# Between two sublayers of a decoder trunk: squares summed on four column groups of TensorE and folded, and the second half's root laid among the first half's features

## The reference, cut to what matters

```python
def rmsnorm(x, g):
    y = x * lax.rsqrt(jnp.mean(x * x, axis=-1, keepdims=True) + NORM_EPS)
    return y * g

x = x + 0.5 * rmsnorm(swiglu(rmsnorm(x, gains[0]), ...), gains[1])
x = x + rmsnorm(mixer(rmsnorm(x, gains[2])), gains[3])
x = x + 0.5 * rmsnorm(swiglu(rmsnorm(x, gains[4]), ...), gains[5])
```

## Time and profile before

| | us |
|---|---|
| median of 3 runs (2783.35 to 2790.81) | 2788.54 |
| the profiled execution | 2786.83 |
| its span | 2785.2 |
| PE busy in it | 2673.0 (96%) |
| DVE busy | 1274.3 (46%) |
| ACT busy | 855.1 (31%) |
| POOL busy | 427.5 (15%) |

### The profile page before, as it was taken

The page is one execution under the profiler, slowest core; times in us unless marked ns, Lnnn a source line. Parts: engine busy times, 40 slices in busy tenths (PEclk is TensorE's granted clock), DMA queues, the critical chain, the costliest instruction groups (busy, mean ns, idle before and its releaser), DMA issues.

```text
span 2785.2 us, 52286 instructions
## 1 busy us (share of the span) xinstructions
PE 2673.0 (96%) x20733; PEld 2511.4 (90%) x20733; DVE 1274.3 (46%) x2112; ACT 855.1 (31%) x1415; POOL 427.5 (15%) x616
## 2 busy tenths in 40 slices
PE   7999999999888999999999999999999889999998
PEld 6999998977444999999899999899999878999998
DVE  5444226554544444432444442468435555544423
ACT  2222223233432332222332232334333233322221
POOL 3000003011443100000100000255144442000001
PEclk9999999999999999999999999999989999999999
DMA  4233322222997222332123333133110114233321
GB/s 116 83 90 88 102 75 69 77 68 72 332 339 264 61 83 84 90 103 84 56 85 89 89 97 94 44 84 83 46 36 1 31 47 129 77 89 90 103 84 43
DMA packets 397671, 263.03 MB, mean 94 GB/s; under 512 B 10954, under 2 KB 370583, under 8 KB 397497
## 3 DMA queue, kind: packets, MB, share of 16 engines
q1 hardware_dynamic: 386012, 223.03, 27.4%
q0 software_dynamic: 11536, 38.28, 4.1%
HBM read 251.71 MB, written 9.56 MB: 94 GB/s over the span
## 4 chain that ended last, share of the span: by engine, by line
PE 90%; DVE 5%; issue 1%; ACT 1%; DMA 1%; POOL 1%; SPq 0%; DVEq 0%; POOLq 0%; ACTq 0%
PE ps L486 67%; PE ps L472 5%; PE ps L2247 2%; PE ps L2268 1%; PE ps L1369 1%; PE ps L2265 1%; PE ps L1381 1%; PE ps L1421 1%; PE ps L500 1%; PE ps L1312 1%; PE ps L1330 1%; PE ps L527 1%; PE ps L1313 1%; PE ps L2231 1%; PE ps L2489 1%
## 5 line engine op out<-in xcount | busy, mean ns | idle before, releaser
L464 DVE TENSOR_TENSOR w_lo<-w_raw,w_hi 128x1024 fp32r<-128x1024 f32 (+1 forms) x314 | 419.8, 1337 | 957.9 <-ACT w_hi L457 956.6
L486 PE MATMUL ps<-hd_hi,w_hi 128*128 128x272 f32 x3712 | 774.7, 290 | 6.0 <-DVE w_lo L464 6.0
L486 PE MATMUL ps<-hd_lo,w_hi 128*128 128x272 f32 x3712 | 767.9, 288 | 0.0
L486 PE MATMUL ps<-hd_hi,w_lo 128*128 128x272 f32 x3712 | 764.1, 287 | 0.0
L457 ACT CAST w_hi<-w_raw 128x1024 fp32r<-128x1024 f32 (+1 forms) x314 | 351.1, 1118 | 1088.6 <-PE ps L486 1023.0
L486 PEld LDWEIGHTS ps<-hd_hi,w_hi 128*128 128x128 f32 x3712 | 581.4, 189 | 14.7 <-issue 14.3
L486 PEld LDWEIGHTS ps<-hd_lo,w_hi 128*128 128x128 f32 x3712 | 584.7, 189 | 0.0
L486 PEld LDWEIGHTS ps<-hd_hi,w_lo 128*128 128x128 f32 x3712 | 582.3, 189 | 0.0
L967 POOL TENSOR_TENSOR xT<-xT,rstd_rows 128x272 f32<-128x272 f32 x96 | 81.0, 871 | 1709.4 <-DVE rstd_rows L992 1709.4
L486 PE MATMUL ps<-h_hi,w_hi 128*128 128x272 f32 x1232 | 255.3, 289 | 0.0
L486 PE MATMUL ps<-h_lo,w_hi 128*128 128x272 f32 x1232 | 254.7, 288 | 0.0
(11 more groups left out here) (500 smaller groups left out, 3175.6 us busy)
## 6 DMA issues: line engine op xcount, KB each, us to landing
w_raw<-in_ffn_w_gate_dram SPq DMA_DIRECT2D x88, 512.0 KB, 3.8
w_raw<-in_ffn_w_up_dram SPq DMA_DIRECT2D x88, 512.0 KB, 3.8
w_raw<-in_ffn_w_down_dram SPq DMA_DIRECT2D x64, 704.0 KB, 4.5
k_pages<-in_cache_a_k_dram SPq DMA_DIRECT2D x128, 256.0 KB, 4.6
v_pages<-in_cache_a_v_dram POOLq DMA_DIRECT2D x128, 256.0 KB, 4.5
w_raw<-in_c_w_in_dram SPq DMA_DIRECT2D x33, 512.0 KB, 4.1
w_raw<-in_ab_w_in_dram SPq DMA_DIRECT2D x25, 512.0 KB, 3.9
w_raw<-in_ab_w_out_dram SPq DMA_DIRECT2D x8, 512.0 KB, 3.7
```

The costliest lines, as they stand in the source:

```text
L464: e.tensor_tensor(w_lo[:, n % 2, 0:nk * P], raw[:, n % RAW, 0:nk * P], w_hi[:, n % 2, 0:nk * P].bitcast(F32), ALU.subtract).then_inc(sem(" ...
L486: mm = e.matmul(ps[:, bank + h, 0:TH], w, x[:, k0 + k, half(h)], start=first and k == 0 and w is wh and x is x_hi, stop=last and k == nk - ...
```

## The change

1. The squares of the new `x` are no longer summed feature by feature by a 128-column product. After features 3 and 7 of a half, four products with 32 columns of ones each go to the four column groups of PE (`ps[j * 32:(j + 1) * 32]`), one for each feature. The four groups' partial sums are copied to scratch by DVE (`dve_sums_out`) and added by one full product (`folded`), after feature 4 of half 1 for half 0, and inside the second unit of half 1 for half 1. The mean divides by 32 times more, since each row of a group is there 32 times.
2. ACT writes squares into six strips instead of two, and waits on PE only at squares 6, 10 and 14 of the 16, and at square 2 for `y_summed` (the strips hold y's squares until then).
3. The last sums of y (`pe_last_sums`) stand in `pe_head`, behind the three passes of feature 0, except after the sixth sublayer.
4. The 12 operations of the second half's root are laid among `scaled` and `x_low` of features 2 to 4 (`dve_rstd_step`), four for each, and wait for each other one by one. Its diagonal stands after `x_low` in feature 5, `pe_rows(1)` after feature 5 instead of 4. This holds for the last turn too.
5. The second unit's `w_hi` stands after feature 4 on ACT and its `w_lo` after feature 6 on DVE.

On DVE, at the first place between sublayers, before: from the `scaled` of feature 4 on (`rstd_rows<-y_ffn` is `scaled`, `hd_lo` is `x_low`, `w_lo` the split of the weights, `small` the root).

```diff
@@ -354,6 +354,10 @@
     return scr[:, x // 2, half(x % 2)]
+def square_strip(h, k):
+    return strip((0, 2, 1, 3, 4, 5)[(h * KD + k) % 6])
@@ -495,10 +499,17 @@
     base = 2 * KD * s
-    def squares(h, k):
-        e.wait_ge(sem("x_squared"), base - 2 * KD + h * KD + k + 1)
-        e.matmul(ps[:, 4 + h, 0:TH], ones[:, :], strip(2 * (k % 2)), start=k == 0, stop=k == KD - 1,
-                 skip_group_check=True).then_inc(sem("squares_summed"), 1)
+    def squares(h, g):
+        e.wait_ge(sem("x_squared"), base - 2 * KD + h * KD + 4 * g + 4)
+        for j in range(4):
+            mm = e.matmul(ps[j * 32:(j + 1) * 32, 4 + h, 0:TH], ones[:, 0:32], square_strip(h, 4 * g + j), start=g == 0,
+                          stop=g == 1, skip_group_check=True)
+        mm.then_inc(sem("squares_summed"), 1)
+    def folded(h):
+        e.wait_ge(sem("sums_copied"), 2 * s - 1 + h)
+        e.matmul(ps[:, 4 + h, 0:TH], ones[:, :], strip(6 + h), start=True, stop=True,
+                 skip_group_check=True).then_inc(sem("squares_folded"), 1)
...
                 if at == 0:
                     e.wait_ge(sem("hd_lo_ready"), base + h * KD + k + 1)
                 mm = pe_passes(e, n, k, hd_hi, hd_lo, k, bank, h, k == 0, k == KD - 1)
-                if at == 0 and s:
-                    squares(h, k)
-                if at == 0 and h == 0 and k == 4 and s:
+                if at == 0 and h == 0 and k == 0 and s:
+                    pe_last_sums(e, s - 1)
+                if at == 0 and k in (3, 7) and s:
+                    squares(h, k // 4)
+                if at == 0 and h == 0 and k == 5 and s:
                     pe_rows(e, s - 1, 1)
+                if h == 1 and at == 0 and k == 4 and s:
+                    folded(0)
+                if h == 1 and at == 1 and k == 3 and s:
+                    folded(1)
             if h == 1:
                 mm.then_inc(sem("unit_done"), 1)
             if h == 1 and at == 0 and between:
@@ -529,6 +546,12 @@
                           skip_group_check=True)
     if last:
         mm.then_inc(sem("y_summed"), 1)
+def pe_last_sums(e, s):
+    g = out_gemm(s)
+    e.wait_ge(sem("y_squared"), y_base[g["name"]] + KD + len(tails_of(g)))
+    pe_sums(e, s, 1, tuple(m % 2 for m in tails_of(g)), False, True)
 def pe_first_rows(e):
@@ -779,8 +802,8 @@
             if h == 1:
                 mm.then_inc(sem("unit_done"), 1)
         mm.then_inc(sem("tail_done"), 1) if h == 0 else None
-    e.wait_ge(sem("y_squared"), y0 + 2 * len(tails_of(g)))
-    pe_sums(e, s, 1, tuple(m % 2 for m in tails_of(g)), False, True)
+    if s + 1 == len(subs):
+        pe_last_sums(e, s)
...
@@ -830,9 +853,11 @@
         act_pre(e, s + 1, 0, 0, 2)
     e.wait_ge(sem("unit_done"), n_end + 4)
     tail(1)
+    if pre:
+        act_pre(e, s + 1, 0, 2, 5)
     act_split(e, n_end + 5, 0, nk_of(n_end + 5))
     if pre:
-        act_pre(e, s + 1, 0, 2, KD)
+        act_pre(e, s + 1, 0, 5, KD)
         act_pre(e, s + 1, 1, 0, KD)
...
...
+def of_rstd_y(h):
+    return (small[:, 6 * x + 3 * h:6 * x + 3 * h + 3] for x in range(3))
 def dve_rstd_y(e, s, h):
     e.wait_ge(sem("y_summed"), 2 * s + h + 1)
-    mean, r_, tmp = (small[:, 6 * x + 3 * h:6 * x + 3 * h + 3] for x in range(3))
+    mean, r_, tmp = of_rstd_y(h)
     chain(e, e.tensor_scalar(mean, ps[:, 4 + h, 0:3], 1.0 / D_MODEL, EPS, ALU.mult, ALU.add))
     dve_rsqrt(e, r_, tmp, mean)
+    dve_diag(e, r_, h)
+def dve_rstd_step(e, s, x):
+    mean, r_, tmp = of_rstd_y(1)
+    if x == 0:
+        e.wait_ge(sem("y_summed"), 2 * s + 2)
+        ins = e.tensor_scalar(mean, ps[:, 5, 0:3], 1.0 / D_MODEL, EPS, ALU.mult, ALU.add)
+    else:
+        e.wait_ge(sem("vector_small"), count["v"])
+    if x == 1:
+        ins = e.tensor_scalar(tmp.bitcast(I32), mean.bitcast(I32), 1, None, ALU.arith_shift_right)
+    if x == 2:
+        ins = e.tensor_scalar(r_.bitcast(I32), tmp.bitcast(I32), -1, MAGIC, ALU.mult, ALU.add)
+    if x >= 3 and x % 3 == 0:
+        ins = e.tensor_tensor(tmp, r_, r_, ALU.mult)
+    if x >= 3 and x % 3 == 1:
+        ins = e.scalar_tensor_tensor(tmp, tmp, -0.5, mean, ALU.mult, ALU.mult)
+    if x >= 3 and x % 3 == 2:
+        ins = e.scalar_tensor_tensor(r_, tmp, 1.5, r_, ALU.add, ALU.mult)
+    count["v"] += 1
+    ins.then_inc(sem("vector_small"), 1)
+def dve_diag(e, r_, h):
     diag = strip(6 + h)
     e.tensor_tensor(diag[:, 0:2 * P].rearrange("p (x n) -> p x n", x=2),
                     ident[:, :].unsqueeze(1).to_broadcast([P, 2, P]),
@@ -913,6 +966,13 @@
     e.tensor_scalar(row_diag[:, SEQ:T], ident[:, 0:NS], r_[:, PT:PT + 1], None, ALU.mult
                     ).then_inc(sem("vector_stage"), reached("row_diag_ready"))
+def dve_sums_out(e, s, h):
+    e.wait_ge(sem("squares_summed"), 4 * s - 2 + 2 * h)
+    if h:
+        e.wait_ge(sem("rstd_spread"), 2 * s)
+    e.tensor_copy(strip(6 + h), ps[:, 4 + h, 0:TH]).then_inc(sem("sums_copied"), 1)
 def dve_rstd_x(e, s, n):
...
@@ -922,9 +982,11 @@
         e.tensor_copy(halves(rb[:, :]), cols(6)).then_inc(sem("mean_ready"), 1)
         e.wait_ge(sem("mean_ready"), 1)
         return
-    e.wait_ge(sem("squares_summed"), 2 * KD * s)
+    dve_sums_out(e, s, 1)
+    e.wait_ge(sem("squares_folded"), 2 * s)
     mean, tmp = scr[:, 2, :], scr[:, 3, :]
-    e.tensor_scalar(halves(mean), cols(4), 1.0 / D_MODEL, EPS, ALU.mult, ALU.add).then_inc(sem("mean_ready"), 1)
+    e.tensor_scalar(halves(mean), cols(4), 1.0 / (32 * D_MODEL), EPS, ALU.mult,
+                    ALU.add).then_inc(sem("mean_ready"), 1)
     dve_split(e, n, 0, KD)
     e.wait_ge(sem("mean_ready"), s + 1)
     e.wait_ge(sem("root_seed"), 2 * s)
@@ -953,10 +1015,12 @@
                      scale=gain(l, n, k)).then_inc(sem("hd_hi_ready"), 1)
         if s == 0:
             continue
-        if s > 1 or h or k >= 2:
-
-            e.wait_ge(sem("squares_summed"), base - 2 * KD + k - 1)
-        e.activation(strip(2 * (k % 2)), xT[:, k, half(h)], ACT.Square).then_inc(sem("x_squared"), 1)
+        q = h * KD + k
+        if q == 2:
+            e.wait_ge(sem("y_summed"), 2 * s)
+        if q >= 6 and q % 4 == 2:
+            e.wait_ge(sem("squares_summed"), 4 * s - 4 + (q - 2) // 4)
+        e.activation(square_strip(h, k), xT[:, k, half(h)], ACT.Square).then_inc(sem("x_squared"), 1)
 def pool_added(e, s):
@@ -992,20 +1056,31 @@
         e.scalar_tensor_tensor(rb[:, half(k % 2)], y[:, k, half(h)], gain(l, n, k), ps[:, 6 + h, 0:TH],
                                ALU.mult, ALU.mult).then_inc(sem("branch_ready"), 1)
+    def step(h, k, x):
+        if h == 0 and 2 <= k < 5:
+            dve_rstd_step(e, s, 4 * (k - 2) + x)
     dve_rstd_y(e, s, 0)
     if pre:
         dve_split(e, n_next, 0, KD)
     scaled(0, 0)
     for h in range(2):
         for k in range(KD):
+            step(h, k, 0)
             if k < KD - 1:
                 scaled(h, k + 1)
+            step(h, k, 1)
+            step(h, k, 2)
             if pre and k:
                 x_low(e, s + 1, *pre_of(s + 1), h, k - 1)
-            if h == 0 and k == 3 and pre:
+            step(h, k, 3)
+            if h == 0 and k == 5:
+                e.wait_ge(sem("vector_small"), count["v"])
+                dve_diag(e, tuple(of_rstd_y(1))[1], 1)
+            if h == 0 and k == 6 and pre:
                 dve_split(e, n_next + 1, 0, KD)
-            if h == 0 and k == 5:
-                dve_rstd_y(e, s, 1)
+            if h == 1 and k == 2 and pre:
+                dve_sums_out(e, s + 1, 0)
         if h == 0:
             scaled(1, 0)
         if pre:
```

## The result

The changed kernel takes 2790.83 us (median, 2786.54 to 2794.98), the kernel before 2785.97 (2781.81 to 2790.81), 20 runs each. The ratio is 1.0018, with a 95% interval of 1.0012 to 1.0024: 0.18% slower, inside the 0.3% that counts as no change. The profiled execution has a span of 2790.0 us against 2785.2.

The account below looks back on a forecast made before the run. Squares and strips on PE were taken to bind each place's second half, DVE the first. Terms 3 x 0.5 + 2 x 1.45 + 2.7 = 7.1 us slower gave 2795 us, own range 2788 to 2802, 8 in 10: 2781 to 2808.

Parts of the forecast that it names:

- The squares, a set at 0.62 us: On PE, four narrow products on 272 columns run side by side and take 0.62 us, bounds 0.5 and 1.84.
- Rival (c): On PE, narrow products don't overlap at 272 columns, each set 1.2 us dearer: 2813 us; chance 0.04.
- the 20 us of my working: PE's list gets back 4.0 us a place, 20 in all: the most the change could bring.
- The root among the features, 11.2 us to the last `x_low`: First half of a place, sums of y to last `x_low`: 8.45 us of DVE work plus 2.75 of meetings.
- The meetings: In the first half, five DVE operations are held by POOL's adds, 0.55 us each: 2.75, bounds 0 and 4.7.
- 8.45 in my sum: DVE's first-half work from the sums to the last `x_low`, without waits beside POOL's adds: 8.45 us.
- rival (a): DVE operations beside POOL's adds cost nothing: 2783.5 us, 2780.5 without the low clock, or 2776.5; chance 0.27.
- Second half 8.7: Last `x_low` of first half to that of second: bound by the features' chain, no longer by PE, 8.7 us.
- The end 5.65: Last `x_low` to body: passes, squares, second unit, fold, mean and `w_lo` take 5.65 us instead of 4.5.
- The places, +0.5 three times and +1.45 twice, 4.4: Between sublayers: first, third and fourth place 0.5 us longer each, second and fifth 1.45 each.
- The last turn +2.7: Last turn: features 3 to 6, root and three held operations take 5.9 us instead of 3.14, 2.7 longer.
- Rival (b), the clock: PE's low clock reaches past 449.4 into the second unit and costs 2.3 us a place: 2807 us; chance 0.14.

Follow-up runs that it names:

- run 9: Kernel before with only the new squares (narrow sets of four, six strips, copies, folds); root, last sums and weight splits as before: 2783.99 us, ratio 0.9990.
- run 3: Changed kernel with the second half's root keeping its running value in PSUM, same order of operations: 2787.09 us, ratio 1.0006.
- run 4: Changed kernel with the root in one block in the last turn only: 2788.47 us, ratio 1.0010.
- run 6: Changed kernel with root's value in PSUM in the places, root in one block in the last turn, and second fold after feature 1: 2783.74 us, ratio 0.9989.
- run 11: The kernel of run 6 measured once more, unchanged: 2782.39 us, ratio 0.9984.
- run 1: Changed kernel with the root in one block behind feature 5, last turn too, and casts and weight splits in their old places: 2794.01 us, ratio 1.0025.
- run 7: Changed kernel with the root's operations one feature later (features 3 to 5), diagonal and `pe_rows` after feature 6: 2802.27 us, ratio 1.0055.
- run 12: The kernel of run 9 with `pe_rows` of the second root after feature 5 instead of 4: 2793.61 us, ratio 1.0024.
- run 5: Changed kernel with the second half's fold after feature 1 of the second unit instead of feature 3: 2788.16 us, ratio 1.0004.
- run 10: The kernel of run 9 with the second half's fold after feature 1 of the second unit: 2780.86 us, ratio 0.9979.
- run 2: Changed kernel with the old squares put back (full products feature by feature, two strips, no folds), root still interleaved: 2795.10 us, ratio 1.0026.

## Why the prediction was right, and by how much

The forecast was "the same, a little slower", by 7.1 us; measured are 4.9 (medians) and 4.8 (spans). The direction and the terms held; the size was over-told by 2.2 us. That the absolute figure of 2795 lies 4.2 above the median is for more than half the base: the 2788.54 of three runs became 2785.97 over twenty.

- **The squares, a set at 0.62 us**: measured 0.59 at full clock (1.06 at 0.50, in the first half). Rival (c) is dead. PE's work fell by 8.1 us of busy time over the five places; the 20 us of my working counted issue slots of a full clock, the busy figures hold the low clock, so the two can't be set against each other. What the squares are worth by themselves, run 9 shows: 0.10%, some 3 us, with an interval that ends at 1.0000; its five places take 2.7 us less from sums to body.
- **The root among the features, 11.2 us to the last `x_low`**: measured 10.9. The meetings are the term that mattered, 5 at 0.55; measured 0.59, 0.60, 0.59, 0.50 and 0.56, sum 2.84 against 2.75. What is left, 8.1 us, was 8.45 in my sum. Run 3 shows the meetings by experiment, and rival (a) falls with it: its root operations of 0.17 us beside an addition appear only where they use PSUM, and then `x_low` pays. The Trainium skill, "SBUF — State Buffer", Who interferes with whom, says that a VectorE instruction with two SBUF inputs is blocked by a GpSimd one that reads SBUF; by that rule each meeting lasts what is left of the addition, and the rows of L938 and L940 agree (0.75 against an addition of 0.76). The first one held (L936) has one input in SBUF and constants, and is held as long; the rule as quoted doesn't cover it.
- **Second half 8.7**: measured 8.35, and for my reason, the features. PE is busy all 8.35 us, but the last `x_low` waits for ACT, which runs without a pause from 449.89 on at 0.93 us a feature, the pace of my sum. In runs 3, 4, 6 and 11, with other first halves and low clocks from 6.8 to 10.2 us, it is 8.33 to 8.45 as well. PE comes out just in step with the last feature (453.80), so there is no room left: where PE was slower, in runs 1, 7 and 12, the second half took 9.5 to 11.0.
- **The end 5.65**: measured 5.89 to 5.99. The set stood 0.24 us later than I counted: the three passes of the last feature took 0.57 us to the set (453.80 to 454.37), not 0.38. That the fold was wanted sooner than it was asked for I had in the sum, but did not see as a fault; runs 5 and 10 show 0.6 to 0.7 us a place in four of the five.
- **The places, +0.5 three times and +1.45 twice, 4.4**: measured 1.95 from sums to body, 1.0 from first `x_low` to body. This term was oversized, the one step of the sum that was far off: both halves were 0.3 us shorter than I counted and the end 0.3 longer, and I gave the third and fourth place the loss of the first though the third took 25.44 us before and not 25.09 (it came out at -0.19). That the second and fifth would lose most was right (+1.12, +0.87).
- **The last turn +2.7**: measured +2.96, with four meetings (0.75, 0.74, 0.75 and the diagonal's 0.73) where I had three. Run 4 takes 1.9 of it back.
- **Rival (b), the clock**: I wrote that it decides once the low clock reaches past 449.4. In after it ends at 445.7, though it lasts 10.2 us instead of 3.4, and is hidden under DVE's first half. A low clock that reaches into the second half is seen in runs 1, 7 and 12, which took 8 to 17 us more than before. What I missed is that `pe_rows` behind feature 5 brings that about when DVE is in time for it, and that the interleaving of the root, by making DVE late, is what hides the late `pe_rows` in the changed kernel (run 3, where DVE is sooner, waits 0.59 us for it). So the two halves of part 4 belong together: the later `pe_rows` alone costs 9.6 us (run 12 against run 9), and after is 2 to 3 us below run 1. The latter has the block in its last turn too, which is worth 1.9 us there (run 4), so in the five places the interleaving gives back more than that; in the traces they take 128.0 us from sums to body with it and 136.5 without.

The net of the change is then the squares (-3 us, run 9) and parts 3 to 5 (+7 us by the ratio of run 2, +8.7 by its medians); their sum of 4 to 6 is near the 4.9 measured. What stays open: how much of the 9.6 us is the clock's and how much the wait's; and whether the interleaved root with `pe_rows` behind feature 4 would do better was not tried.

## What to carry to other kernels

In this kernel a small chain of dependent VectorE operations was cheapest in a block while GpSimd stood idle; spread among GpSimd's additions, it or the operation behind it paid for each of them. When work is taken off TensorE between two stages, look in the trace at where its clock comes back: the same slot of a small product made VectorE wait 0.26 us at full clock and 1.13 at half. A busy engine need not be the bound: ask what the last instruction of a stage waited for. And test each half of a two-part change alone: here the squares were a gain of 0.1% (0.2% with an earlier fold) hidden under the loss of the root's new order.
